# A decoder step on one core: the order of the input stage, and the gate at the end moved to VectorE

## What is computed

```python
mod = silu(c) @ ada_w + ada_b                       # c: 1 prompt row and 8 sample rows
sh1, sc1, g1, sh2, sc2, g2 = split(mod, 6)
h = rmsnorm(x, norm1_g) * (1 + sc1) + sh1
z = h @ w_in                                        # columns q | k | v | u
att = dilated_attention(q, k, v, cache, rel_bias)   # 8 heads x 64
ssm = s5_branch(u, state, ...)                      # scan over positions, GELU, GLU
x = x + g1 * (concat(rmsnorm(att), rmsnorm(ssm)) @ w_out)
h2 = rmsnorm(x, norm2_g) * (1 + sc2) + sh2
x = x + g2 * hier_moe(h2, ...)                      # top-1 of 4 groups, top-2 of 4 experts
y = rmsnorm(x, final_norm_g)
```

## Time and profile before

| | us |
|---|---|
| timed runs, median (lowest to highest) | 845.99 (845.0 to 846.4) |
| the profiled execution, own time | 843.27 |
| its span | 841.3 |
| TensorE busy | 667.7 (79%) |
| VectorE busy | 290.3 (35%) |
| ScalarE busy | 177.0 (21%) |
| GpSimd busy | 141.1 (17%) |
| DMA, mean over the span | 252 GB/s |
| chain that ended last | PE 64%, DMA 11%, DVE 10%, SPq 7%, issue 4%, ACT 3% |

### The profile page before, as it was taken

One profiled execution on the slowest core, in us unless ns is written; L12 is line 12 of the kernel. 1 busy time (PEld: TensorE's weight loads), 2 busy tenths in 40 slices (PEclk: granted clock), 3 DMA queues, 4 the chain that ended last, 5 costly groups with the idle time before them and its releaser, 6 DMA issues.

```text
span 841.3 us, 11928 instructions
## 1 busy us (share of the span) xinstructions
PE 667.7 (79%) x4846; PEld 385.6 (46%) x4846; DVE 290.3 (35%) x686; ACT 177.0 (21%) x362; POOL 141.1 (17%) x229
## 2 busy tenths in 40 slices
PE   2196999999999775999994389877899999989600
PEld 1165887888873342444554244322344444333200
DVE  4848196762111442424555611100010111100048
ACT  3222311122224464421211001100110101100132
POOL 4300004657600132100000000000000000000072
PEclk9567999999999998999995589988899999999955
DMA  9945348584693998894119268999998459999362
GB/s 338 256 172 202 104 155 306 160 280 140 205 196 142 392 282 219 327 381 184 55 43 334 92 209 301 336 391 407 396 350 296 181 174 394 393 401 401 160 212 106
DMA packets 92908, 211.86 MB, mean 252 GB/s; under 512 B 8540, under 2 KB 15084, under 8 KB 92565
## 3 DMA queue, kind: packets, MB, share of 16 engines
q1 hardware_dynamic: 81878, 182.48, 61.6%
q0 software_dynamic: 4976, 18.37, 7.3%
q10 hardware_dynamic: 6000, 10.25, 3.3%
HBM read 197.42 MB, written 18.91 MB: 257 GB/s over the span
## 4 chain that ended last, share of the span: by engine, by line
PE 64%; DMA 11%; DVE 10%; SPq 7%; issue 4%; ACT 3%; POOL 1%; ACTq 0%; DVEq 0%; POOLq 0%
PE ps L2420 14%; PE ps L2044 11%; PE ps L2460 9%; PE ps L2326 7%; SPq L635 6%; DMA whalf<-in_w_down 5%; PE ps L1933 5%; DMA ring<-in_cache_v 4%; PE ps L2014 4%; PE ps L1939 2%; PE ps L2157 1%; PE ps L2132 1%; PE ps L1984 1%; DMA const<-in_const 1%; PE ps L2179 1%
## 5 line engine op out<-in xcount | busy, mean ns | idle before, releaser
L2420 PE MATMUL ps<-whalf,xgT 128*128 128x512 f32 (+2 forms) x576 | 176.3, 628 | 14.5 <-DMA whalf<-in_w_up 10.0
L2420 PEld LDWEIGHTS ps<-whalf,xgT 128*128 128x128 f32 (+2 forms) x576 | 67.8, 160 | 115.2 <-issue 110.3
L2460 PE MATMUL ps<-whalf,aT 128*128 128x512 f32 (+2 forms) x288 | 88.7, 643 | 12.8 <-DMA whalf<-in_w_down 11.0
L2044 PE MATMUL ps<-hT,ring 128*128 128x272 f32 x384 | 91.4, 394 | 0.0
L2044 PEld LDWEIGHTS ps<-hT,ring 128*128 128x128 f32 x384 | 71.8, 190 | 15.2 <-issue 1.4
L2460 PEld LDWEIGHTS ps<-whalf,aT 128*128 128x128 f32 (+2 forms) x288 | 33.6, 162 | 60.9 <-issue 58.5
L2326 PE MATMUL ps<-ring,mixT 128*128 128x512 f32 x128 | 58.1, 610 | 1.9 <-ACT mixT L812 1.9
L778 POOL DMA_INDIRECT xg<-h_d,gidx x12 | 11.5, 955 | 244.1 <-PE ps L1933 206.4
L762 POOL TENSOR_TENSOR Sb<-Sb,stat 128x128 f32<-128x128 f32 (+3 forms) x32 | 22.3, 719 | 111.3 <-DVE stat L1579 111.3
L1828 DVE COPY ysb<-ps 128x512 f32<-128x512 f32 x12 | 8.3, 692 | 92.5 <-PE ps L2460 92.5
L1815 DVE SCALAR_TENSOR_TENSOR a_s<-a_t,ps 128x512 f32<-128x512 f32 x12 | 8.3, 688 | 89.5 <-ACT a_t L812 89.5
(11 more groups left out here) (396 smaller groups left out, 940.6 us busy)
## 6 DMA issues: line engine op xcount, KB each, us to landing
whalf<-in_w_down SPq DMA_DIRECT2D x32, 1024.0 KB, 16.0
whalf<-in_w_gate SPq DMA_DIRECT2D x32, 1024.0 KB, 10.1
whalf<-in_w_up SPq DMA_DIRECT2D x32, 1024.0 KB, 15.0
ada_half<-in_ada_w SPq DMA_DIRECT2D x16, 1024.0 KB, 5.3
ring<-in_cache_k SPq DMA_DIRECT2D x8, 1792.0 KB, 8.0
ring<-in_cache_v SPq DMA_DIRECT2D x6, 2048.0 KB, 12.0
ring<-in_ada_w SPq DMA_DIRECT2D x4, 2048.0 KB, 16.8
ring<-in_w_in SPq DMA_DIRECT2D x4, 2048.0 KB, 10.9
```

Source lines behind the costliest of these rows:

```text
L2044: ins = mm(ps[:, z % 2, 0:2 * NCOL], r[:, 512 * k + P * (c % 4):512 * k + P * (c % 4 + 1)], hT[:, k, 2 * h:2 * h + 2, :].rearrange("p a b ...
L2420: ins = mm(out[cols, :], xgT[b][:, k, cols], r[:, 512 * (k % 4):512 * (k % 4 + 1)], start=k == 0, stop=k == KD - 1, **tile_at(m_, n))
L2460: ins = mm(ps[cols, 6 + n2, :], aT[:, t % 2, c, cols], r[:, c0:c0 + 512], start=c == 0, stop=c == 3, **tile_at(m_, n))
```

## The change

It reorders the input stage on every engine and moves two pieces of the end. SP loads x in two parts, with only the identity columns of const, ahead of a0; the modulation rows that are needed first (0 to 3 and the gains) come behind a0; ct_re, ct_im, oh_decode, the rest of const, the other modulation rows and h0 come behind U. VectorE and ScalarE scale x before the parameter chain, and the modulation chunks stand inside that chain. The decode bias, the turning of bpad and `km_in` move behind `u_in(3)`; bpad moves onto the area of x. At the end VectorE does the gate, and GpSimd waits for the y stores itself.

```diff
@@ names of semaphore values
-CS, GSB, DBIAS, HMD, CQ3, CQ4, TABLES, KMD, SQ1, SQ2, SQ3, SSN = range(1, 13)
-GP, DBP, MODTP, ATTSP = range(1, 5)
+CS, GSB, HMD, CQ3, CQ4, DBIAS, TABLES, KMD, SQ1, SQ2, SQ3, SSN = range(1, 13)
+GP, MODTP, DBP, ATTSP = range(1, 5)
...
-    bpad = [at("bpad_re", [P, STT, P], TAB), at("bpad_im", [P, STT, P], TAB + 8192)]
+    bpad = [at("bpad_re", [P, STT, P], QK), at("bpad_im", [P, STT, P], QK + 8192)]
@@ SP
+        def modrows(a, b, done):
+            for j in range(4):
+                sp.dma_start(modrow[32 * j:32 * j + 32, a:b, :].rearrange("p a b -> p (a b)"),
+                             I["modrow"][j, P * a:P * b].partition_broadcast(32)).then_inc(done, 16)
+        n0 = CCOL["ident"][1]
         sp.dma_start(cT[:, :, :], I["cT"]).then_inc(s("cld"), 16)
-        sp.dma_start(par[:, :], I["par"]).then_inc(s("init"), 16)
-        fill("a0", ada_col(0))
+        sp.dma_start(par[:, :], I["par"]).then_inc(s("parl"), 16)
         sp.dma_start(ctab33[:, :], I["tab33"]).then_inc(s("init"), 16)
         sp.dma_start(ohp[:, :], I["oh_prompt"]).then_inc(s("init"), 16)
-        sp.dma_start(const[:, :], I["const"]).then_inc(s("init"), 16)
-        sp.dma_start(xt[:, 0:QT, :], xq_v).then_inc(s("x"), 16)
+        sp.dma_start(const[:, 0:n0], I["const"][:, 0:n0]).then_inc(s("x0"), 16)
+        sp.dma_start(xt[:, 0:2, :], xq_v[:, 0:2, :]).then_inc(s("x0"), 16)
+        sp.dma_start(xt[:, 2:QT, :], xq_v[:, 2:QT, :]).then_inc(s("x"), 16)
         sp.dma_start(xt[0:NS, QT, :], I["x"][SEQ:NTOK, :]).then_inc(s("x"), 16)
+        fill("a0", ada_col(0))
+        modrows(0, 4, s("modl"))
+        modrows(N_ADA, N_ADA + 4, s("modl"))
         fill("a1", ada_col(1))
+        fill("a2", ada_col(2))
+        sp.wait_ge(s("ada"), 1)
+        fill("a3", ada_col(3))
+        sp.wait_ge(s("ada"), 2)
+        fill("U", win_col(3))
         for n, name in enumerate(("ct_re", "ct_im")):
             sp.dma_start(cq[n][:, :, 0, :], I[name]).then_inc(s("ctl"), 16)
         sp.dma_start(oh[:, :], I["oh_decode"]).then_inc(s("ctl"), 16)
...
+        sp.dma_start(const[:, n0:], I["const"][:, n0:]).then_inc(s("ctl"), 16)
+        modrows(4, N_ADA, s("ctl"))
         sp.dma_start(h0[:, 0, :, :], I["h0_re"]).then_inc(s("h0"), 16)
         sp.dma_start(h0[:, 1, :, :], I["h0_im"]).then_inc(s("h0"), 16)
-        sp.wait_ge(s("ada"), 2)
-        fill("U", win_col(3))
@@ GpSimd
-        for b in range(2):
-            o(pool.memset(bpad[b][:, :, :], 0.0))
...
+        pool.wait_ge(s("hTp"), 2 * NT)
+        for b in range(2):
+            o(pool.memset(bpad[b][:, :, :], 0.0))
...
-        pool.wait_ge(s("y_all"), 1)
+        for u in range(2):
+            pool.wait_ge(s_yst[u], 16 * ((NREG + 1 - u) // 2))
...
-        for j in range(NT):
-            w = TW[j]
-            g2 = g2P[0:w, :] if j < QT else mod3S[0:w, 0, :]
-            pool.wait_ge(s("endld"), 96)
-            pool.wait_ge(s("ysum"), j + 1)
-            a = yg[0:w, j, 0, :]
-            pool.tensor_tensor(a, a, g2, ALU.mult).then_inc(s("ygate"), 1)
@@ ScalarE
         for j in range(NT):
-            raw_half(j)
-        for n in range(8):
...
+            if j == 0:
+                act.wait_ge(s("x0"), 32)
+            if j == 2:
+                act.wait_ge(s("x"), 32)
+            w = TW[j]
+            f(xsq[0:w, :], xt[0:w, j, :], ACT.Square,
+              accum_out=stat[0:w, j:j + 1]).then_inc(s("sq"), 1)
+            act.wait_ge(s("sq"), j + 1)
+            root(j, j + 1, w, D).then_inc(s("rt"), 1)
+            if j >= 2:
+                raw_half(j - 2)
+        raw_half(NT - 2)
+        raw_half(NT - 1)
...
         mod_chunk(4)
-        km_out()
         u_out(2)
         u_out(3)
         mod_chunk(5)
+        for n in range(8):
+            b, q = n // 4, n % 4
+            act.wait_ge(s("btT"), n + 1)
...
         mod_store(4)
+        km_out()
@@ VectorE (rstd, raw_half, mod_chunk as before, moved up)
         ts_(q_(4), q_(4), 3.1415925, -3.1415925, ALU.min, ALU.max).then_inc(s("par_dve"), 1)
+        dve.wait_ge(s("pe_prep"), GP)
...
+        for j in range(NT):
+            w = TW[j]
+            rstd(j, w, D, j + 1)
...
+        raw_half(NT - 1)
...
+        mod_chunk(0)
         dve.wait_ge(s("par_act"), 5)
...
+        mod_chunk(1)
         for m in range(1, CT):
...
+            if m == 1:
+                mod_chunk(2)
+                mod_chunk(3)
+                feature_mod()
...
+        dve.wait_ge(s("ctl"), 128)
         o(ts_(cq[1][:, :, 0, :], cq[1][:, :, 0, :], -1.0, None, ALU.mult))
-        mod_chunk(1)
         next_cq(1)
-        mod_chunk(2)
         next_cq(2)
...
-        dve.wait_ge(s("kmp"), 4)
-        dve.wait_ge(s("pool_prep"), BPAD)
         for z in range(7):
+            if z == 5:
+                dve.wait_ge(s("pe_prep"), DBP)
+                o(v.tensor_copy(dbias[:, :], ps[:, 6:8, :].rearrange("p a b -> p (a b)")[:, 0:DK]))
...
+        def gate(j):
+            w = TW[j]
+            a = yg[0:w, j, 0, :]
+            if j == 0:
+                dve.wait_ge(s("endld"), 96)
+            dve.wait_ge(s("ysum"), j + 1)
+            tt_(a, a, g2P[0:w, :] if j < QT else mod3S[0:w, 0, :], ALU.mult).then_inc(s("ygate"), 1)
...
         weigh(0)
-        weigh(1)
         for j in range(NT):
+            gate(j)
+            if j + 1 < NT:
+                weigh(j + 1)
             residual(j)
-            if j + 2 < NT:
-                weigh(j + 2)
@@ TensorE
         pe.wait_ge(s("dve_prep"), CS)
+        h_t(0)
+        h_t(1)
         ada(0)
-        for j in range(NT):
-            h_t(j)
+        h_t(2)
+        h_t(3)
+        h_t(4)
         ada(1)
...
+        ada(2)
+        ada(3)
...
         u_in(0)
         ada_half(0)
         u_in(1)
         ada_half(1)
+        u_in(2)
+        ada_half(2)
+        u_in(3)
+        ada_half(3)
+        dec_bias()
+        bp_t()
         km_in()
-        for b in range(2, 6):
-            u_in(b)
-            ada_half(b)
+        u_in(4)
+        ada_half(4)
+        u_in(5)
+        ada_half(5)
```

More of the change, by code:

```diff
@@ L681, in _ @@
         pool.sem_inc(s("pool_prep"), 1)
-        pool.wait_ge(s("modl"), 64)
+        pool.wait_ge(s("modl"), 128)
+        pool.wait_ge(s("ctl"), 128)
         def mod_chunk(c):
@@ L789, in _ @@
                 gather(NREG + 2 * i + 1)
-        pool.wait_ge(s("y_all"), 1)
+                for u in range(2):
+                    pool.wait_ge(s_yst[(NREG + u) % 2], 16 * ((NREG + 2 * i + u) // 2 + 1))
+        for u in range(2):
+            pool.wait_ge(s_yst[u], 16 * ((NREG + 1 - u) // 2))
         for j in range(NT):
@@ L1238, in _ @@
         f(stat[0:1, 62:63], epst[0:1, :], ACT.Sqrt)
-        for u in range(2):
-            act.wait_ge(s_yst[u], 16 * pairs + 16 * ((NREG + 1 - u) // 2))
-        act.sem_inc(s("y_all"), 1)
         def scale_first(j):
@@ L1294, in _, with rstd, raw_half @@
         ts_(q_(4), q_(4), 3.1415925, -3.1415925, ALU.min, ALU.max).then_inc(s("par_dve"), 1)
+        dve.wait_ge(s("pe_prep"), GP)
+        v.tensor_copy(gsb[:, :], ps[0:HEADS, 6:8, :].rearrange("p a b -> p (a b)")[:, 0:640]).then_inc(s("dve_prep"), 1)
+        def rstd(j, w, width, n):
+            dve.wait_ge(s("sq"), n)
+            dve.wait_ge(s("rt"), n)
+            o(v.reciprocal(stat[0:w, 56 + j:57 + j], stat[0:w, 16 + j:17 + j]))
+        def raw_half(j):
+            dve.wait_ge(s("hTp"), 2 * j + 2)
+            bank = ps[:, 3 + 2 * (j % 2), 0:4 * TW[j]]
+            if j < QT:
+                ins = v.tensor_copy(hT[:, 4:8, j, NSEQ:NCOL], bank.rearrange("p (a b) -> p a b", a=4))
+            else:
+                for k in range(4):
+                    ins = v.tensor_copy(hT[:, 4 + k, :, 0:NSEQ].rearrange("p j n -> p n j"),
+                                        bank[:, NS * k:NS * (k + 1)].rearrange("p (n j) -> p n j", j=TDEC))
+            ins.then_inc(s("hTd"), 1)
@@ new lines, in _, with mod_chunk @@
+        for j in range(NT):
+            w = TW[j]
+            rstd(j, w, D, j + 1)
+            ts_(xt[0:w, j, :], xt[0:w, j, :], stat[0:w, 56 + j:57 + j], None, ALU.mult).then_inc(s("h"), 1)
+            if j:
+                raw_half(j - 1)
+        raw_half(NT - 1)
+        def mod_chunk(c):
+            dve.wait_ge(s("ada"), c + 1)
+            if c == 0:
+                dve.wait_ge(s("modl"), 128)
+            m = modsb[:, c, :]
+            if c < 2:
+                tt_(m, ps[:, c % 2, 0:P], modrow[:, c, :], ALU.add).then_inc(s("modd"), 1)
+            else:
+                o(stt(out=m, in0=ps[:, c % 2, 0:P], scalar=1.0, in1=modrow[:, c, :], op0=ALU.add, op1=ALU.add))
+                tt_(m, m, modrow[:, N_ADA + c % 2, :], ALU.mult).then_inc(s("modd"), 1)
@@ new lines, in feature_mod @@
+        def feature_mod():
+            dve.wait_ge(s("act_prep"), MODT)
+            dve.wait_ge(s("hTa"), NT)
+            dve.wait_ge(s("hTd"), NT)
+            for k in range(4, KD):
```

(24 more changed lines are left out.)

106 lines of the change are left out of this document (13 added, 93 removed).

## The result

The changed kernel takes **831.81 us** (830.8 to 832.56, four runs), the kernel before on the same chip 845.5 (840.12 to 846.4, four runs): a ratio of 0.9854, interval 0.9828 to 0.9879. That is 13.7 us less where 16.0 had been forecast, and 1.8 us above the forecast of 830.0. The profiled execution took 830.8 us; before it was 843.27.

The account below looks back on a forecast made before the run. TensorE was taken to bound most of the span. Head 34.1 - 16.1 - 5 - 2 = 11.0 plus tail 5.0 gave 16.0 us off 843.27, 827.3; with 2.7 for the median, 830.0 us, range 816 to 838.5.

Parts of the forecast that it names:

- u's start: Head, TensorE: the first u product comes at 42.3 us against 76.44, 34.1 us less; bounds 40.5 and 46.
- a3's landing: Head, load queue: 11.6 MB up to the end of a3 at 385 GB/s, so a3 lands at 32.8 us.
- The moved pieces: Decode bias and bpad turning, now between u(3) and u(4) on TensorE: 16.1 us, or 11.6 at full clock.
- The new wait: TensorE stands about 5 us ahead of ada_half(0), then 2 us more for u(1) at half clock; bounds together 0 and 14.
- x_in(0): End of the head on TensorE: 11.0 us earlier, near 114.3 us where it was 125.28.
- The tail: From the gathers to the last norm: gathers 1.2 us earlier, gates moved to VectorE; 5.0 us gained, bounds 2.5 and 6.5.
- The middle: From x_in(0) to the first gather: stays at 673 us, the head's gain handed on one for one; otherwise the prediction is wrong.
- (a): Rival, head: no new wait arises and the bias runs at full clock; head gains 22.5, time 818.5 us; chance 0.17.
- (b): Rival, SP queue: h0's issue again takes 9.91 us, TensorE stands 13 us and not 5; 838 us; chance 0.14.
- (c): Rival, tail: the last three gathers each locked out for one VectorE operation; tail gains 2.1, time 832.9 us; chance 0.10.
- (d): Rival: the cache_v load's wait swallows the head's 11 us, as its stream doesn't start earlier; 841 us; chance 0.05.
- (e): Rival: slower, the first ada_half landing from about 72 us on; at 76 us the time is 850 us; chance 0.04.

Follow-up runs that it names:

- e6: The changed kernel with the decode bias and the turning of bpad back ahead of the first u product, loads left in their new order: 836.33 us.
- e2: The changed kernel with the old end, so the new input stage alone: 835.12 us, ratio 0.9916 to the kernel before.
- e4: The changed kernel with the eight small modulation row transfers issued behind a1 instead of behind a0: 831.86 us.
- e5: The changed kernel with three of the four terms of the decode bias product left out, so its decode attention is not the reference's: 823.49 us.
- e3: The changed kernel with the first two ada_half transfers issued right behind U, ahead of ct_re, ct_im and the other small loads: 829.22 us.
- e0: The changed kernel itself, unaltered, run once more: 831.7 us, ratio 0.9863 to the kernel before.
- e1: The kernel before with only the new end (gates on VectorE, GpSimd waiting for the y stores itself), input stage untouched: 839.45 us.

## Why the prediction was right, and where not

**u's start: 42.3 forecast, 46.0 measured** (45.3 and 45.4 in the other two profiles). The failed term is a3's landing, put at 32.8 and found at 37.2 (issue at 21.62, 15.6 us to land); in all three profiles ada(3) starts within 0.2 us of it. The sum by bytes took 385 GB/s from 2.6 us on and blocks that arrive whole in turn. The engines moved 371 from 6 to 37 us, and a0 to a3 and U were under way together, so that each block's last packet came late (a0 at 17.9, a1 25.1, a2 31.8, a3 37.2, U 42.5). At 335 GB/s over the whole 37.2 us they had moved 12.5 MB, 0.9 more than the 11.6 reckoned: by that estimate 2.3 of the 4.4 us. That this part is U's is argued from the landings, no run took it apart. ada(3) ran at the low clock (3.59 us for its 64 products, 3.3 taken). 46 was the upper bound.

VectorE was late as well, and nearly the next limit: mod_chunk(1) was out at 36.59 where 33.7 was forecast, 0.6 us ahead of a3. (In the other two profiles VectorE came to its chain 3 us earlier, and it was out at 33.67 and 33.58.) The chain that took 7.8 us before (14.63 to 22.40) now took 9.9 (26.40 to 36.30). The change had put GpSimd's clearing of bpad, two memsets of 1.80 us, beside it, and two of its operations stretched: the copy of sth, 0.18 us in the earlier trace rows and 1.26 now, and the one that makes cth, 0.17 before and 1.62 now. Each ended with one of the memsets (at 27.66 and 27.62, at 29.52 and 29.48). The same pair is as long in the other two profiles. VectorE's and GpSimd's timelines:

```profile
26.40 1.26 DVE L1359 COPY sth<-pr 128x16 f32<-128x16 f32 x1
...
27.68 1.80 POOL L683 MEMSET bpad_im<- 128x2048 f32 x1
27.90 1.62 DVE L1361 TENSOR_SCALAR cth<-pr 128x16 f32<-128x16 f32 x1
```

**The moved pieces: 16.1 forecast, 13.5 measured** (11.6 would have been the full clock's). The term was taken whole from a stretch of which much was at half clock. The bias product alone takes 6.86, 10.02 and 7.81 us in three profiles of the same kernel. It is the granted clock that makes the difference: from its start to the next product it is 6.80, 9.95 and 7.74 us at a mean clock of 0.94, 0.64 and 0.82, and length times clock is 6.4 us each time, as in the kernel before (9.81 at 0.65) and in e6 (12.70 at 0.50). In the first profile the clock was 1.00 in the first half of it and 0.88 in the second:

```profile
86.00:89.30 3.30, 3.30 (x9) 1.31 (x7) 0.00 (x0) 0.00 (x0) 0.00 (x0) 0.88 0.33 128
```

So a price read from one execution carried some 3 us of chance in it, and it was no rule that they "came behind full clock, as they will now".

**The new wait: 5 + 2 us forecast, 1.68 us measured** (2.27 and 2.12 in the other profiles; 3.6 us in e2, e4 and e5, where u began 2.0 to 2.3 us earlier). The landing, forecast at 54.7 to 56, came at 57.1. Since u itself began 3.7 us late, most of the wait was hidden by it: these two errors are one and nearly cancel. The clock behind the wait was 1.00 (57 to 61 us) and not half. The half clock came later instead, behind a gap of 2.31 us at 64.90.

**A term that the sum lacked: gaps in TensorE's own issue.** They come to 3.7, 4.2 and 3.9 us in the u stage of the changed kernel's three profiles, and to 1.4 and 1.1 in the two of the kernel before. The profile names no semaphore for them, but they stand at fixed places in TensorE's program. Counted in recorded products, those of 0.3 us and more in the first 110 us fall behind the 475th, 603rd, 731st, 986th, 1114th or 1369th, that is 127 to 128 apart or twice that, in all 14 profiles; only how many of these places show one, and how long it is, differs. (Two other idle times without a releaser are left out: 0.73 us ahead of km_in and e6's 14.47.) And each of these 37 gaps ended 1.2 to 1.6 us after a packet of 16,384 bytes had landed on the queue q8, of the kind "instruction", by the packet records of the trace; the page gives only their sum, 39 packets and 0.64 MB (in the changed kernel a packet landed at 65.98, and the gap of 2.31 us ended at 67.22; in e3 at 58.07 and 59.30). So by these times TensorE waited there for its own instructions. No run changed their loading, and why some of these packets come late isn't shown.

**x_in(0): 114.3 forecast; 112.3, 117.9, 114.0 measured**, and before 125.3 and 123.5. The head's gain by the middle profiles is 10.4 us (11.0 forecast); the head alone measured 8.3 by runs. In the first profile u's late start (+3.7) stood against the shorter wait and bias (-5.3 and -2.6), and the gap (+2.3) took a part back: 112.4. Four errors of 2.3 to 5.3 us left 1.9 between them, so that the forecast came so near is in part luck. Against the first profile, e0 lost 2.2 us ahead of the bias and 3.3 in the moved pieces, and the third 0.2 and 1.4: gaps and the clock together spread x_in(0).

**The tail: 5.0 forecast, 4.8 in the traces, 4.0 by the runs of e1.** Its steps held: the 2.96 us stand was foreseen, and 36.1 us became 36.4. One step failed in size: the earlier start of the gathers, put at 1.2 us, is 0.6 (the last copy of ysb to the first gather: 4.80 us before, 4.19 after), and 0.6 is what GpSimd's own wait gives. (The store had landed at 796.92 and the gathers started 1.40 us later; after, it landed at 789.05 and they started 0.78 later.) No run took the gates and this wait apart.

**The middle: handed on one for one, as forecast.** The prediction had named as a sign of being wrong that the time from x_in(0) to the first gather isn't the 673 us of before; it was 677.5 in the first profile (673.6 and 674.9 in the other two, and 676.8 in the second of the kernel before). So the first pair of traces spoke against it by 5.1 us in the middle, but the second profile of the kernel before has 672.0 us there, and those of the change 669.4 and 670.7: one for one within some 3 us, no closer. The forecast's base execution happened to hold 668.2. That base had been 2.7 us under the median, and the prediction added those back, which covered what the trace didn't tell.

**The rivals.** (a) lies 13.3 us below the measured time: the wait was there and the bias, though faster than taken, not at the full clock. (b) falls: h0's issue was held 0.42 us, not 9.91. (c) falls: the last three gathers took 1.28, 0.96 and 1.34 us where the undisturbed take 0.94, so all of them together lost 0.8 us, not 3.6; VectorE's operations beside them were 1.2 to 1.3 us. The prediction left out the conditions of the rule of the Trainium skill (SBUF — State Buffer, section "SBUF: two separate sides"): there the loser is held back for the whole instruction when VectorE's operation is in a 2-port mode, or has two SBUF inputs while GpSimd's reads SBUF, and starved descriptors belong to the first of these. VectorE's operations beside the gathers have two SBUF inputs, and a gather reads its indices from SBUF; if it counts as the second case, the trace doesn't agree, for none lost a whole operation. Of the starving these rows are no test. The gates are the second case without question, and there the trace agrees: beside them the residual took 3.37 us, and with them off GpSimd (e1) 1.21. (d) falls: the wait for cache_v is 33.72 us, as it was, and it starts 11.3 us earlier. (e) would have needed a landing at 72 us; it came at 57.1.

## What to carry to other kernels

Put first on a queue what the longest chain of small operations needs, and let its big loads run behind it: here that bought 8 to 10 us although 13.5 us of TensorE work were only moved. Price a moved stretch from two executions at least where the granted clock in it isn't 1.00, or take its length times the clock as the price at full clock; and sum from a middle execution, not from one that happens to be at hand. When a piece moves on one engine, look at what the other engines do at its new time: beside GpSimd's memsets two operations of VectorE's chain took 2.5 us longer here. When operations are put in order for several tiles, let the one that waits for another engine go one tile later; that was worth 3.4 us of tail here, nearly as much as the gates.

## What the runs showed of the hardware that had not been expected

- TensorE's granted clock is low or falls in continuous work too: 12.00 of 12.00 us busy at 0.50 in e6, from a standstill, and 0.77 to 0.83 in a stretch that had 1.00 in another execution of the same program. The same 16 records took 6.86, 7.81, 10.02 and 12.71 us, and length times clock, to the start of the next product, was 6.4 us in each.
- By the times of the packets, TensorE waits for its own instructions: gaps of 0.3 to 2.7 us between independent products, at the same places of its program in each kernel, each ending 1.2 to 1.6 us after a 16,384-byte packet of the instruction queue had landed (37 of 37 in the first 110 us of 14 profiles).
- Two operations of VectorE on 128x16 elements, 0.18 and 0.17 us before, took 1.26 and 1.62 us beside GpSimd's memsets of 1.80 us.
- The same issue of ct_re held SP 9.26 us at the start, 5.37 us behind U and 2.24 us behind the first two halves as well (e3); h0's, of the same size each time, 9.91 and 0.42 us.
